# Page numbers for the cache reads held in SBUF, read from there by the sync engine

## The chip, the cores and the metric

The kernel runs on one core of a Trainium2 chip. The metric is the time of the whole program on the device, in microseconds, as the median of several runs. The engines are named as in the profile: PE (matrix products; PEld its weight loads), DVE (vector), ACT (scalar), POOL (general purpose) and SP (sync, which here does nothing but wait and issue DMAs; its rows carry the name SPq). Sixteen DMA engines move the data.

## The reference, cut to what matters

A two-layer decoder trunk works on 256 prompt tokens and 8 sample tokens with the same weights. In each layer a normalised input is projected by one wide matrix; one branch is a state space scan, the other latent attention; their gated sum goes through `w_out`, and a retrieval of single-neuron experts (PEER) follows. What matters here is the attention of the samples, each of which reads 2048 past positions out of a paged cache:

```python
past_lat = cache_latent[l][page_table].reshape(bs, past_len, KV_LORA)
past_kr = cache_krope[l][page_table].reshape(bs, past_len, QK_ROPE)
...
s = (jnp.einsum('bqhr,btr->bhqt', ql, kv) + jnp.einsum('bqhd,btd->bhqt', qp, kr)).astype(jnp.float32) * ATTN_SCALE
p = jax.nn.softmax(jnp.where(mask, s, -jnp.inf), axis=-1).astype(kv.dtype)
return jnp.einsum('bhqt,btr->bqhr', p, kv)
```

`page_table` has 8 rows (samples) of 16 page numbers, int32, in HBM. It is the same for both layers.

## The kernel before

A first block loads the constants, the inputs and a norm row, and all engines meet at a barrier. Then a loop over the two layers runs, each layer one block in which the five engines go through programs written out by hand and meet only by semaphores. So on each engine the order of the code is the order of execution.

**The sync engine's program of a layer.** It issues the loads of all weights into `wring`, a ring of two blocks: `load_block` waits on `blocks_begun`, which PE raises with the first product of each block, since the block before it is then no longer read. `block_of(w_in, GATE_B, k)` loads the last four of the input projection's 1 MB blocks; between them stand the first cache reads. The past of a sample is read in two halves, so there are `HALVES` = 16 of them, of `HALF_PAGES` = 8 pages each. A page is one DMA of 128 rows of 2176 bytes (272 KB) into `held`, a part of `arena` with three slots (`HELD` = 3); half i goes into slot i % 3. Before its eight DMAs `half_numbers(i)` reads the half's eight page numbers into registers of the sync engine, and for i from 3 on the engine then waits until PE has done the values of half i - 3, which frees the slot:

```python
for i in range(HELD, HALVES):
    if i in SSM_LOADS:
        block_of(w_ssm, 0, SSM_LOADS[i])
    numbers = half_numbers(i)
    sp.wait_ge(sem("aux_full"), marks["values", i - HELD])
    half_pages(i, numbers)
```

Half 0 begins after the wait on `el_used` (with the gate blocks), half 1 follows, and half 2 begins after the wait on `ring_free`, when the arena's last user before attention is done. The registers are loaded from HBM: the compiled program has, for each half, a load of the table's address (shown as `in_page_table_ptr`), a register addition where the half isn't the first, and one load of the eight numbers (`in_page_table`). These are the rows of L2027; the page DMAs are L2034, the weight blocks L2003.

**PE in the same stretch.** It does the gate products (L485 from `ht_tok,wring`), some turns and products, and then for each half `half_scores(i)` (L861 and L865, after the half's pages have landed), pieces of prompt attention and of the SSM projection (L485 from `arena,wring`), and `half_values(i)` (L886). Then come the attention's output products, `w_out`, and PEER, whose rows POOL gathers by indirect DMA (L2154) in a stretch of some 690 us per layer. POOL also moves the samples' SSM states in and out (L2126, L2132) while PE does the gate products.

Of the kernel before, what the change touches and what calls it, by code (L numbers as in the profile page):

```python
# [11 lines left out]
I32 = mybir.dt.int32  # L12
U32 = mybir.dt.uint32

D_MODEL, SEQ, DEPTH, SAMPLES = 1024, 256, 2, 8
# [5 lines left out]
PAGES = PAST // PAGE  # L21
# [26 lines left out]
HALF_PAGES = PAGES // 2  # L48
# [232 lines left out]
def build(nc, layers, a, out):  # L281

    (o_yp, o_ys, o_latp, o_krp, o_ssmp, o_convp, o_lats, o_krs, o_ssms, o_convs) = out
    a = dict(a, next_norm=a["norms"][1:DEPTH + 1, :])
    with ExitStack() as ctx:
        def sb(name, cols, dt=F32):
            return ctx.enter_context(nc.sbuf_tensor(name, [P, cols], dt))
# [3 lines left out]
        def sem(name):  # L291
            if name not in sems:
                sems[name] = ctx.enter_context(nc.semaphore(name))
            return sems[name]
# [48 lines left out]
        ysm = sb("ysm", DC * SAMPLES)  # L343
        att = sb("att", 96)
        layer_off = sb("layer_off", 2)
        arena = sb("arena", max(A1 + 2048, A3))
        ps = ctx.enter_context(nc.psum_tensor("ps", [P, 8, 512], F32))

# [99 lines left out]
        with nc.Block() as block:  # L448
            @block.sync
            def _(sp):  # L450
                sp.dma_start(consts[:, :], a["consts"]).then_inc(sem("first_loads"), 16)
                sp.dma_start(x[:, 0:2, :], a["x_prompt"].rearrange("o (t p) d -> p (o t) d", p=P)).then_inc(sem("first_loads"), 16)

                sp.dma_start(nrow[:, :], a["norms"][0, :].partition_broadcast(P)).then_inc(sem("first_loads"), 16)
                sp.wait_ge(sem("x_zeroed"), 1)
                sp.dma_start(x[0:SAMPLES, 2, :], a["x_sample"].rearrange("b o d -> (b o) d")).then_inc(sem("first_loads"), 16)
                sp.wait_ge(sem("first_loads"), 16 * 4)

            @block.vector
            def _(dve):  # L460
                dve.memset(x[:, 2, :], 0.0).then_inc(sem("x_zeroed"), 1)
                dve.memset(fwd[:, :], 0.0)
                dve.memset(layer_off[:, :], 0.0).then_inc(sem("off_zeroed"), 1)
# [3 lines left out]
        with nc.Fori(0, layers) as layer:  # L467
            with nc.Block() as block:
# [1525 lines left out]
                def _(sp):  # L1994
# [28 lines left out]

                    def half_numbers(i):

                        s = i // 2
                        return nc.values_load_multi_w_load_instructions(  # L2027
                            a["page_table"][s:s + 1, (i % 2) * HALF_PAGES:(i % 2 + 1) * HALF_PAGES], engines=(mybir.EngineType.SP,),
                            min_val=0, max_val=a["pages"].shape[1] - 1, skip_runtime_bounds_check_because="page numbers lie in the pool")[1]

                    def half_pages(i, numbers, some=range(HALF_PAGES)):
# [25 lines left out]
                    block_of(w_in, GATE_B, 1)  # L2057
                    sp.wait_ge(sem("el_used"), 1)
                    numbers = half_numbers(0)
                    half_pages(0, numbers, range(0, 2))  # L2060
                    half_pages(0, numbers, range(2, 4))
                    block_of(w_in, GATE_B, 2)
                    half_pages(0, numbers, range(4, 6))
                    block_of(w_in, GATE_B, 3)
                    half_pages(0, numbers, range(6, 8))
                    half_pages(1, half_numbers(1))
                    block_of(w_ssm, 0, 0)
                    sp.wait_ge(sem("ring_free"), 1)
                    half_pages(2, half_numbers(2))
# [4 lines that stand above are left out]
# [176 lines left out]
```

## Time and profile before

| | |
|---|---|
| median of 3 runs | 2316.95 us (2314.4 to 2320.23) |
| the profiled execution's own time | 2312.3 us, of which the span of the profile is 2310.8 us |
| PE busy | 1953.5 us, 85% of the span |
| DVE busy | 1516.2 us, 66% |
| DMA | 744.48 MB, mean 322 GB/s |
| page reads | 256 DMAs of 272 KB, 128 per layer |

The profile is of one execution, 4.65 us shorter than the median. Layer 0 lies at about 10 to 1160 us of the span and layer 1 at 1160 to 2300 us; the gate products with the first page reads at 186 to 222 us and 1330 to 1366 us, and the sixteen halves at 261 to 392 us and 1404 to 1534 us.

### The profile page before, as it was taken

The numbers are of one execution on the slowest core, as the hardware profiler recorded it, in microseconds if no ns is written. First come the engines' busy times: TensorE is split into PE (matmuls) and PEld (weight loads), VectorE is DVE, ScalarE is ACT, GpSimd is POOL, SyncE is SP. The second block draws the span as 40 slices with busy tenths as digits, with TensorE's granted clock in tenths as the row PEclk, the third lists the DMA queues.
The fourth block names the chain that finished last, engine by engine and source line by source line (L and its number), as shares of the span: only waits on it lengthen the run. The fifth ranks groups of instructions, "written<-read, shape, count | busy, mean of one in ns | idle before, by whom it ended". The sixth has DMA issues, their size and how long they took to land. (4 is left out here: it accounts for less than half of the span.)

```text
span 2310.8 us, 26923 instructions
## 1 busy us (share of the span) xinstructions
PE 1953.5 (85%) x9174; PEld 1124.3 (49%) x9174; DVE 1516.2 (66%) x3832; ACT 458.5 (20%) x1378; POOL 643.0 (28%) x594
## 2 busy tenths in 40 slices
PE   7999888999898777777699998899988987787775
PEld 5887656744344322222278876566544442222221
DVE  3555434677787888788545544337678778888874
ACT  2244210122112111111022532101121121111111
POOL 0000000134444344445200000002344443544451
PEclk9999899999999999999999999999999999999998
DMA  5447489499999999999654466875999998999995
GB/s 187 149 133 260 137 289 323 146 398 417 421 421 420 419 368 422 421 421 411 291 183 136 146 223 206 275 272 207 398 416 421 421 421 370 419 421 421 421 414 240
DMA packets 188196, 744.48 MB, mean 322 GB/s; under 512 B 16338, under 2 KB 76170, under 8 KB 117376
## 3 DMA queue, kind: packets, MB, share of 16 engines
q0 software_dynamic: 83296, 582.18, 61.5%
q1 hardware_dynamic: 104752, 160.47, 20.7%
q8 instruction: 74, 1.21, 0.2%
q14 instruction: 74, 0.61, 0.1%
HBM read 731.33 MB, written 11.46 MB: 321 GB/s over the span
## 5 line engine op out<-in xcount | busy, mean ns | idle before, releaser
L1067 PE MATMUL ps<-arena 128*128 128x512 f32 (+1 forms) x2112 | 1013.8, 613 | 238.7 <-DVE arena L1645 232.9
L2154 POOL DMA_INDIRECT arena<-in_peer_uv,arena x528 | 607.9, 1151 | 864.7 <-PE ps L1067 704.3
L1636 DVE CUSTOM_DVE_ANT_0 arena<-arena,h 128x1024 f32<-128x1024 f32 x512 | 627.5, 1226 | 236.2 <-DMA arena<-in_peer_uv,arena 228.9
L1067 PEld LDWEIGHTS ps<-arena 128*128 128x128 f32 (+1 forms) x2112 | 366.4, 188 | 849.0 <-DVE arena L1645 529.2
L485 PE MATMUL ps<-ht_tok,wring 128*128 128x264 f32 (+2 forms) x1728 | 380.8, 377 | 8.8 <-DMA wring<-in_w_in 5.4
L485 PEld LDWEIGHTS ps<-ht_tok,wring 128*128 128x128 f32 x1728 | 312.3, 190 | 75.2 <-issue 18.2
L1950 ACT ACTIVATE arena<-arena 128x1 f32<-128x1 f32 x528 | 105.8, 203 | 1031.3 <-DVE arena L1636 1030.5
L1645 DVE TENSOR_SCALAR arena<-consts,arena 128x128 f32<-128x128 f32 (+1 forms) x528 | 181.6, 344 | 20.6 <-ACT arena L1950 20.6
L2135 POOL DMA_DIRECT2D nrow<-in_norm_ffn x2 | 1.1, 533 | 334.2 <-PE ps L824 334.2
L485 PE MATMUL ps<-arena,wring 128*128 128x264 f32 (+2 forms) x512 | 91.8, 336 | 0.8 <-DVE arena L1420 0.8
L485 PEld LDWEIGHTS ps<-arena,wring 128*128 128x128 f32 x512 | 77.0, 191 | 10.3 <-DVE arena L1420 1.3
L494 PE MATMUL ps<-consts,h 128*128 128x128 f32 (+2 forms) x174 | 36.2, 315 | 31.4 <-DVE h L1165 27.8
L485 PE MATMUL ps<-wring,ht_tok 128*128 128x272 f32 (+5 forms) x288 | 59.4, 365 | 0.0
L485 PE MATMUL ps<-arena,gate 128*128 128x256 f32 x256 | 57.2, 382 | 2.2 <-DVE gate L1427 2.2
L886 PE MATMUL ps<-arena 128*32 128x256 f32 x512 | 36.0, 401 | 21.0 <-DVEq L1445 21.0
L485 PEld LDWEIGHTS ps<-arena,gate 128*128 128x128 f32 x256 | 48.1, 191 | 9.5 <-DVE gate L1427 2.6
L1292 DVE SCALAR_TENSOR_TENSOR h<-h,exs,arena 128x1024 f32<-128x1024 f32 x16 | 20.6, 1285 | 49.0 <-ACT arena L1825 49.0
L494 PEld LDWEIGHTS ps<-consts,h 128*128 128x128 f32 (+2 forms) x174 | 26.4, 173 | 48.8 <-DVE h L1165 29.4
L2126 POOL DMA_DIRECT2D out<-h x16 | 8.5, 534 | 148.9 <-DVE h L1292 148.9
L485 PEld LDWEIGHTS ps<-wring,ht_tok 128*128 128x128 f32 (+1 forms) x288 | 42.2, 161 | 15.6 <-issue 2.6
L861 PE MATMUL ps<-arena 128*32 128x256 f32 x512 | 37.1, 411 | 11.5 <-DVEq L1370 6.0
L1950 ACT ACT_TABLE_LOAD x36 | 46.2, 1283 | 0.6
(319 smaller groups left out, 1744.7 us busy)
## 6 DMA issues: line engine op xcount, KB each, us to landing
arena<-in_pages SPq DMA_DIRECT2D x256, 272.0 KB, 4.0
wring<-in_w_in SPq DMA_DIRECT2D x38, 1024.0 KB, 5.9
wring<-in_peer_wq SPq DMA_DIRECT2D x18, 1024.0 KB, 9.5
arena<-in_peer_uv,arena POOLq DMA_INDIRECT x528, 12.5
h<-in_state_ssm POOLq DMA_DIRECT2D x16, 512.0 KB, 5.1
out<-h POOLq DMA_DIRECT2D x16, 512.0 KB, 5.0
wring<-in_w_ssm_proj SPq DMA_DIRECT2D x8, 1024.0 KB, 8.2
arena<-in_w_out SPq DMA_DIRECT2D x8, 1024.0 KB, 14.9
```

Source lines behind the costliest of these rows:

```text
L485: last = pe.matmul(dst, w(c), rhs(c), start=start and c == 0, stop=stop and c == chunks - 1)
L494: return pe.transpose(dst, src, ident[0:rows, 0:rows])
L861: pe.matmul(ps[32 * g:32 * g + 32, b, 0:256], qs[:, s, c, :], held[:, slot, 2 * g:2 * g + 2, c * P:(c + 1) * P], start=c == 0, stop=False, ...
L886: last = pe.matmul(ps[32 * g:32 * g + 32, b, 0:KV_LORA], pts[:, i % 2, j, g, :], held[:, slot, 2 * g + j, 2 * P + ROPE:KV_ROW], start=j == ...
L1067: last = pe.matmul(ps[0:outs, SUM_BANK[t] + half, :], diag[:, n % DIAGS, 0:outs], ring[:, HOME[n % RING], D_MODEL + half * 512:D_MODEL + ( ...
L1292: dve.scalar_tensor_tensor(out=new, in0=new, scalar=exs[:, SAMPLES + s:SAMPLES + s + 1], in1=stx[:, s % 2, :, :], op0=ALU.mult, op1=ALU.ad ...
L1636: dve.tensor_tensor_reduce(ring[:, HOME[k], 0:D_MODEL], ring[:, HOME[k], 0:D_MODEL], tokens, 1.0, 0.0, ALU.mult, ALU.add, dots[:, column(n ...
L1645: dve.tensor_scalar(diag[:, n % DIAGS, 0:outs], table[:, 0:outs], gel[:, column(n)], wexp[:, column(n)], ALU.mult, ALU.mult).then_inc(sem( ...
L1950: act.activation(gel[:, at:at + 1], dots[:, at:at + 1], ACT.Gelu).then_inc(sem("gelu_ready"), 1)
L2126: pool.dma_start(h1[b], places[b % PLACES]).then_inc(sem(f"state_store{b % PLACES}"), 16)
L2135: pool.dma_start(nrow[:, :], of_layer("norm_ffn", layer).partition_broadcast(P)).then_inc(sem("ffn_row_load"), 16)
L2154: pool.indirect_dma_start(ring[:, HOME[k], :], None, table, bass.IndirectOffsetOnAxis(ap=idx[:, TOPK * u + j:TOPK * u + j + 1], axis=0)).t ...
```

## The change

The kernel gets an SBUF tensor `numbers` of 128 int32 per partition, of which partition 0 is used. The first block loads the whole page table (128 numbers, 512 bytes) into it by one more DMA, ahead of the samples' input, and waits for it with the other first loads. `half_numbers(i)` reads its eight numbers from SBUF.

```diff
+        numbers_held = sb("numbers", SAMPLES * PAGES, I32)
         arena = sb("arena", max(A1 + 2048, A3))
...
                 sp.dma_start(nrow[:, :], a["norms"][0, :].partition_broadcast(P)).then_inc(sem("first_loads"), 16)
+                sp.dma_start(numbers_held[0:1, :], a["page_table"].rearrange("(o s) k -> o (s k)", o=1)).then_inc(sem("first_loads"), 16)
                 sp.wait_ge(sem("x_zeroed"), 1)
                 sp.dma_start(x[0:SAMPLES, 2, :], a["x_sample"].rearrange("b o d -> (b o) d")).then_inc(sem("first_loads"), 16)
-                sp.wait_ge(sem("first_loads"), 16 * 4)
+                sp.wait_ge(sem("first_loads"), 16 * 5)
...
                     def half_numbers(i):
 
-                        s = i // 2
                         return nc.values_load_multi_w_load_instructions(
-                            a["page_table"][s:s + 1, (i % 2) * HALF_PAGES:(i % 2 + 1) * HALF_PAGES], engines=(mybir.EngineType.SP,),
+                            numbers_held[0:1, i * HALF_PAGES:(i + 1) * HALF_PAGES], engines=(mybir.EngineType.SP,),
```

What the sync engine's program holds in the first block, before (`ISA` in such listings is a short register instruction, `DMA` the issue of a transfer):

```order
L451 DMA consts<-in_consts 128x1428
L452 DMA x<-in_x_prompt 128x2x1024
L454 DMA nrow<-in_norms 128x1024
L456 DMA x<-in_x_sample 8x1024 [waits x_zeroed]
L448 UNCONDITIONAL_BRANCH [waits first_loads]
```

and with the change:

```order
L452 DMA consts<-in_consts 128x1428
L453 DMA x<-in_x_prompt 128x2x1024
L455 DMA nrow<-in_norms 128x1024
L456 DMA numbers<-in_page_table 1x128
L458 DMA x<-in_x_sample 8x1024 [waits x_zeroed]
L449 UNCONDITIONAL_BRANCH [waits first_loads]
```

One DMA issue stands ahead of the samples' input. The other place is the step from one half to the next on the sync engine, here from the last page of half 2 to the first of half 3, before:

```order
L2034 DMA arena<-in_pages 128x544
L2027 TENSOR_LOAD in_page_table_ptr
L2027 REGISTER_ALU
L2027 TENSOR_LOAD in_page_table
L2034 ISA [waits aux_full]
```

and with the change:

```order
L2035 DMA arena<-in_pages 128x544
L2028 TENSOR_LOAD numbers
L2035 ISA [waits aux_full]
```

Two loads and an addition have become one load, in each of 32 such steps. On the other engines nothing has moved.

## Rows read from the trace of the kernel before

**Rows 1.** The page: DMA share in tenths, 40 slices of the span

```profile
DMA  5447489499999999999654466875999998999995
```

**Rows 2.** PE's waits for transfers (us, times, longest): 186:222, 1330:1366, 185:410, 1404:1534

```profile
PE ps L485 <- DMA wring<-in_w_in: 3.1, 1, 3.1
...
PE ps L485 <- DMA wring<-in_w_in: 2.1, 1, 2.1
...
PE ps L861 <- DMA arena<-in_pages: 4.2, 3, 1.7
...
PE ps L861 <- DMA arena<-in_pages: 1.2, 2, 0.9
```

**Rows 3.** The sync engine's waits, whole span

```profile
SPq L2034 <- PE ps L886: 0.5, 1, 0.5
```

**Rows 4.** L2027, whole span: duration ns min/median/max, first and last start

```profile
L2027 SPq TENSOR_LOAD <-in_page_table_ptr x32: 832/2522/4115, 190.0 to 1512.6; - x32
L2027 SPq TENSOR_LOAD <-in_page_table x32: 887/899/2475, 192.6 to 1514.5; - x32
L2027 SPq ALU_OP  x30: 37/38/58, 212.9 to 1514.5; - x30
```

**Rows 5.** L2027 in 189:194, 215:264, 264:272 and 280:287

```profile
L2027 SPq TENSOR_LOAD <-in_page_table_ptr x1: 2591/2591/2591, 190.0 to 190.0; - x1
...
L2027 SPq TENSOR_LOAD <-in_page_table_ptr x1: 837/837/837, 258.0 to 258.0; - x1
...
L2027 SPq TENSOR_LOAD <-in_page_table_ptr x1: 2652/2652/2652, 264.5 to 264.5; - x1
L2027 SPq TENSOR_LOAD <-in_page_table x1: 893/893/893, 267.3 to 267.3; - x1
...
L2027 SPq TENSOR_LOAD <-in_page_table_ptr x1: 3933/3933/3933, 281.8 to 281.8; - x1
```

**Rows 6.** Sync engine's timeline: half 3 alone; halves 2 to 4; half 3's landing

```profile
268.40 4.67 SPq L2034 DMA_DIRECT2D arena<-in_pages  x8
...
260.20 20.96 SPq L2034 DMA_DIRECT2D arena<-in_pages  x24
...
DMA to landing us min/median/max: 2.7/3.9/5.0
```

**Rows 7.** DMA in stretches: us, busy of five engines, PEclk, DMA share, GB/s

```profile
193.00:195.00 2.00, 2.00 (x10) 1.72 (x10) 0.71 (x1) 1.18 (x5) 0.00 (x0) 1.00 0.44 114
201.00:206.00 5.00, 2.78 (x13) 2.05 (x11) 3.65 (x3) 1.56 (x6) 1.06 (x2) 1.00 1.05 361
...
276.00:278.00 2.00, 2.00 (x60) 1.48 (x52) 0.82 (x2) 0.00 (x0) 0.00 (x0) 1.00 0.36 100
...
2.00:8.00 6.00, 0.00 (x0) 0.00 (x0) 0.47 (x3) 0.00 (x0) 0.00 (x0) 1.00 1.01 366
```

**Rows 8.** Sync engine's timeline, 185:330, at the gate blocks

```profile
188.59 0.54 SPq L2003 DMA_DIRECT2D wring<-in_w_in  x1
193.80 2.04 SPq L2034 DMA_DIRECT2D arena<-in_pages  x4
196.50 0.56 SPq L2003 DMA_DIRECT2D wring<-in_w_in  x1
```

**Rows 9.** PE's timeline: start, us, what, [idle before, ended by]; both layers

```profile
280.95 1.05 PE L861 MATMUL ps<-arena 128*32 128x256 f32 x16
...
305.14 1.07 PE L861 MATMUL ps<-arena 128*32 128x256 f32 x16 [1.73 <-DMA arena<-in_pages]
...
383.39 1.07 PE L861 MATMUL ps<-arena 128*32 128x256 f32 x16 [1.70 <-DMA arena<-in_pages]
...
391.48 0.39 PE L911 MATMUL ps<-arena,latt 128*8 128x64 f32 x4
...
1525.36 1.07 PE L861 MATMUL ps<-arena 128*32 128x256 f32 x16 [0.29 <-DMA arena<-in_pages]
...
1533.44 0.39 PE L911 MATMUL ps<-arena,latt 128*8 128x64 f32 x4
```

## The prediction

> **What bounds the kernel now.** I read the page first. The DMA share is 9 in the long gather stretches of PEER and in the attention slices of both layers [rows 1]. The change touches nothing in PEER, so the question is what the sync engine's page reads cost PE. The list of waits, cut to the stages, answers it: PE waits for pages 4.2 us in layer 0 (three times, 1.7 at most, at halves 6, 8 and 15; the first of these is in [rows 9]) and 1.2 us in layer 1, and once per layer for a gate block of `w_in`, 3.1 and 2.1 us, at the place where page reads stand between the weight loads [rows 2]. Together that is 5.4 + 5.2 = 10.6 us. This is the most that page reads can give back, 0.46% of the time.
>
> Why do pages come late? The sync engine's own waits show it: for a slot to be freed it waited once in the whole run, 0.5 us [rows 3]. In all other steps the slot had been free, and the engine itself came late. Its timeline says with what: eight page issues take 4.67 us, but three halves take 20.96 us from first issue to last, so two steps of (20.96 - 3 x 4.6) / 2, about 3.6 us, lie between them [rows 6]. They are the register loads: a median of 2.52 us for the address, 0.04 for the addition and 0.90 for the numbers, with gaps 3.6 [rows 4].
>
> Is a wait of PE passed on to the end? Half 15 began after a wait of 1.70 us in layer 0 and of 0.29 us in layer 1, and from there to L911 behind the last half it took 8.09 us (391.48 - 383.39) and 8.08 us (1533.44 - 1525.36) [rows 9]. So nothing behind the wait had used it. After attention everything hangs on PE's products until the first expert numbers, and the gathers follow from them. I pass it on one to one.
>
> **The change part by part.**
>
> *The load's new length.* It is not in this trace; bounds come from the loads that are. The address load took 0.84 us after the engine's long wait for `ring_free`, 2.65 us right behind eight page issues, and 3.93 us behind a 1 MB weight block; the numbers load that followed the second of these, from the same memory under the same traffic, took 0.89 us [rows 5]. So it isn't the reading that is long but being the first read behind DMA issues: about 1.7 us of it looks like a wait until those issues have got through. The new load is now the first read. Lower bound 0 (an SBUF read might cost next to nothing and wait for nothing), upper bound 4.1 us, the longest address load [rows 4]. I take 2.5 us behind pages, the address load's median, because it takes that load's place, and 0.84 after idleness. Then a step saves the second load, the addition and their gaps, 1.0 us of 3.6; with a load of 0.84 it would save 2.8.
>
> The Trainium skill's page "DMA: Bandwidth & Descriptors", section "Latency and other measured facts", gives HBM access 0.2 us on average and 2 us at high load, and a floor of some 600 ns for such a register load. By it the first load would be long because HBM is busy, and one from SBUF would be back in 0.6 us, saving 3.0 us a step; the sum below would stay, and the last two rivals would lose most of their chance. The trace disagrees as to the cause: the second load reads HBM just as busy and takes 0.89 [rows 5].
>
> *What an earlier issue gains in attention.* The DMA engines set a floor. Half 3 was issued from 268.40 on; its last page landed 5.0 us after an issue near 272.7, so at about 277.7, while half 4's first issue was at about 276.9 (one period of 8.5 later). Between them the engines idled: in 276 to 278 us their share was 0.36, so 1.3 us of idleness in a period of 8.5, [rows 6, 7]. With the idleness gone a half needs 7.2 us. A 1 MB weight block at 361 GB/s [rows 7] adds 2.9 us, and three of them stand among halves 3 to 15. PE, without its waits, goes from half 3 to half 15 in 383.39 - 280.95 - 4.2 = 98.2 us [rows 2, 9]. The engines' floor for the same twelve steps is 12 x 7.2 + 3 x 2.9 = 95.1 us, and half 3 already lies there 3.2 us ahead of PE (280.95 - 277.7). So the floor is below PE's need by 6 us at the end; the tightest places are halves 6 and 8, behind weight blocks. Half 6 could have landed at 277.7 + 3 x 7.2 + 2.9 = 302.2 and is wanted at 305.14 - 1.73 = 303.4 [rows 9]: 1.2 us are left. The lead must also be made: one microsecond saved per step gives 3 to 4 by half 6, where 1.7 is wanted, and more than 10 by half 15, where 4.2 is; some is lost in waiting for slots at halves 3 and 4. So I expect nearly all of the page waits to go: 5.0 of 5.4 us. What is late next in those places is DVE's part between the products, which stands in the trace anyway and moves along with PE.
>
> *The gate blocks.* The block issued at 196.50 is the one PE waits for 3.1 us. Its issue hangs on PE's own start of a block, and I leave it there; what can change is how much is queued ahead of it. Four pages are issued ahead of it from 193.80 on, after the loads that begin at 190.0 [rows 5, 8]. In 193 to 195 us the DMA share is 0.44, so 1.1 us of engine time is lost there, and until the block has landed the engines are full (1.05 in 201 to 206) [rows 7]. Pages issued 1.0 us earlier fill this hole and let the block land that much earlier; more than 1.1 us can't be won, as the previous block's transfer lies before it, unless the full stretch shortens by other means. Bounds: 0 and 3.1 us in layer 0, 0 and 2.1 in layer 1. I take 1.15 each, 2.3 us.
>
> *The added DMA.* One more issue, about 0.5 us, stands ahead of the samples' input. In 2 to 8 us the engines are full with the constants and the prompt (1.01) [rows 7], and the input's 32 KB comes behind them in any case, so the cover is 5 us deep; 512 bytes more are nothing. 0 us, and 0.5 if the cover were gone. The new tensor moves the arena by 512 bytes per partition, 0.
>
> **Sum:** 5.0 + 2.3 - 0 = 7.3 us. The profiled execution's own time of 2312.3 us becomes 2305.0. The median of the runs shown is 4.65 us above it, and I give the time on that scale: 2316.95 - 7.3 = 2309.7 us, 0.31% less.
>
> **The rivals.**
>
> 1. *The gate waits go as a whole.* Then 5.4 + 5.2 = 10.6 us, 2306.4. For it: the load may be back 1.7 us sooner than I take. Against it: only 1.1 us of idle engine time lies there [rows 7]. Chance 0.13.
> 2. *The DMA floor catches the gain.* Pages issued sooner only queue longer; one or two waits behind weight blocks stay, and POOL's state transfers take the hole ahead of the gate block. For it: 6 us of slack in 98, about 1 at halves 6 and 8. Then 3 to 5 us, 2312 to 2314. Chance 0.22.
> 3. *The change doesn't shorten the step.* If the new load returns only when the pages have passed, at the moment the numbers load returns now, nothing is won: 2317. For it: the first load's length follows what was issued ahead of it; against it: in each case shown the numbers load takes its own 0.9 on top. Chance 0.08.
> 4. *Slower: the load from SBUF takes longer than the whole step does now*, because it competes with page writes into the same memory. It decides from 3.6 us on. Every period is already the sync engine's, so 4.1 us, the upper bound, costs 0.5 x 12 steps x 2 layers = 12 us: 2329. For it only that the reading side isn't in the trace; against it the 0.84 and 0.89 us of plain reads. Chance 0.07.
>
> **How the numbers follow.** My forecast has 0.50, with 5.5 to 9 us. From no change this kernel can be told by about 0.3%, 7 us. Rival 1 and somewhat over half of the forecast's chance lie beyond: faster 0.45. The rest of the forecast with rivals 2 and 3 is the same: 0.48. Rival 4 is slower: 0.07. The range leaves out rival 4 and most of rival 3: from rival 1 less 1 us, 2305.5, to 2316.0. The forecast's own is 2307.5 to 2312.
>
> **What would show it.** In the profile after: one register load per half, about 2.5 us behind pages and 0.8 at half 2; the step between halves about 2.6 instead of 3.6 us. SP waits for slots (L2035 for PE) not once but in many halves, several us in all. PE's waits for pages under 0.5 us, for the gate block about 2 and 1 us. The first barrier at the same time. The DMA share between halves up from 0.36. I am wrong if the load is over 3.6 us, if waits for pages stay at halves 6 and 8, or if the time falls by less than the waits do, so that something behind attention had the slack.

## The result, and the profile after

| | before | after |
|---|---|---|
| median of four runs | 2316.01 us (2314.4 to 2320.23) | 2297.77 us (2289.79 to 2302.48) |
| ratio | | 0.9905, 95% interval 0.9884 to 0.9925 |
| profiled execution, span | 2310.8 us | 2288.3 us |
| mean granted clock of that execution | 0.980 | 0.985 |

The kernel became faster by 18 us; forecast were 7.3. The profiled execution is the fastest of the four and 8 us below their median, so its 22.5 us of difference in span are more than the change typically gives.

The register loads come first. The groups of L2028, whole span, with duration in ns as min/median/max; they answer to [rows 4]:

```profile
L2028 SPq TENSOR_LOAD <-numbers x32: 521/526/735, 189.2 to 1486.0; - x32
```

One load of 0.53 us stands where there were 2.52 + 0.04 + 0.90 and their gaps. From the end of half 0's last page issue to the start of half 1's first, both layers show 0.78 us. Even right behind page issues the load is short. The longest, 0.735 us, is the very first.

What the sync engine and PE wait for (us in total, times, longest), the first two over the whole span, the last two in 186:222 and 1320:1366:

```profile
SPq L2035 <- PE ps L888: 65.5, 24, 5.3
...
SPq L449 <- DMA x<-in_x_sample: 6.3, 1, 6.3
...
PE ps L487 <- DMA wring<-in_w_in: 1.0, 1, 1.0
...
PE ps L487 <- DMA wring<-in_w_in: 0.7, 1, 0.7
```

The sync engine waited for a slot once and 0.5 us before [rows 3]; now it waits 24 times and 65.5 us: it runs ahead of PE. PE has no wait for pages left in either layer, where it had 4.2 and 1.2 us, and its gate-block waits fell from 3.1 and 2.1 us [rows 2] to 1.0 and 0.7. The 10.6 us of waits for transfers in these places are now 1.7. The first barrier's wait is no longer than before (6.3 us against 6.5).

At the gate blocks, the sync engine's timeline (start, us), and then DMA in stretches (us, busy of five engines, PEclk, DMA share, GB/s):

```profile
187.80 0.54 SPq L2005 DMA_DIRECT2D wring<-in_w_in  x1
190.20 2.04 SPq L2035 DMA_DIRECT2D arena<-in_pages  x4
195.70 0.56 SPq L2005 DMA_DIRECT2D wring<-in_w_in  x1
```

```profile
193.00:195.00 2.00, 2.00 (x11) 1.71 (x10) 1.41 (x2) 0.38 (x2) 0.00 (x0) 1.00 1.05 390
...
2.00:8.00 6.00, 0.00 (x0) 0.00 (x0) 0.48 (x3) 0.00 (x0) 0.00 (x0) 1.00 0.99 367
```

The four pages begin 3.6 us earlier than in [rows 8] (the whole program is 0.8 us ahead here), and the hole of share 0.44 [rows 7] is filled: 1.05. The block that PE waits for is issued 0.8 us earlier, as PE itself is, and comes sooner: from its issue to PE's first product with it 10.4 us passed before (196.50 to 206.88) and 8.3 after (195.70 to 204.01).

These waits are 8.9 us. The other part of the difference has its own sign in the trace. PE between gates and attention, before and then after (start, us, what, [idle before, ended by]):

```profile
231.03 5.45 PE L494 MATMUL ps<-consts,arena 128*128 128x128 f32 x24 [1.87 <-DVEq L1326]
236.41 7.31 PE L485 MATMUL ps<-cqt,arena 128*128 128x264 f32 x24
```

```profile
228.16 4.25 PE L496 MATMUL ps<-consts,arena 128*128 128x128 f32 x24 [1.87 <-DVEq L1328]
232.34 5.61 PE L487 MATMUL ps<-cqt,arena 128*128 128x264 f32 x24
```

The same products take 2.9 us less, with no transfer near. The row of a stretch of before says why: the granted clock was 0.50, the lower of its two levels, 1.2 instead of 2.4 GHz, with PE busy throughout:

```profile
233.10:239.90 6.80, 6.80 (x21) 4.64 (x22) 2.62 (x7) 3.82 (x7) 0.00 (x0) 0.50 0.00 0
```

So two things changed: waits for transfers, and time at the lower clock. The experiments ask whether the second belongs to the change, and through what.

### The profile page after: what moved, and what is told of

The parts are those of the page before. It is cut to its first block and busy times, and to the rows that moved or that the text cites. A ratio compares the mean times of both kernels' runs of the same rounds, so it can differ in the third digit from the quotient of the medians.

```text
span 2288.3 us, 26862 instructions
## 1 busy us (share of the span) xinstructions
PE 1941.2 (85%) x9174; PEld 1117.7 (49%) x9174; DVE 1516.4 (66%) x3832; ACT 458.8 (20%) x1378; POOL 648.7 (28%) x594
## 5 line engine op out<-in xcount | busy, mean ns | idle before, releaser
L888 PE MATMUL ps<-arena 128*32 128x256 f32 x512 | 35.8, 399 | 21.0 <-DVEq L1447 21.0
L487 PEld LDWEIGHTS ps<-wring,ht_tok 128*128 128x128 f32 (+1 forms) x288 | 41.2, 158 | 15.3 <-issue 2.6
L1945 ACT ACT_TABLE_LOAD x34 | 43.6, 1283 | 0.8
```

The source lines that it names most:

```text
L487: last = pe.matmul(dst, w(c), rhs(c), start=start and c == 0, stop=stop and c == chunks - 1)
L888: last = pe.matmul(ps[32 * g:32 * g + 32, b, 0:KV_LORA], pts[:, i % 2, j, g, :], held[:, slot, 2 * g + j, 2 * P + ROPE:KV_ROW], start=j == ...
L1945: act.activation(w, w, ACT.Exp, accum_out=wsum[:, u % 2:u % 2 + 1]).then_inc(sem("experts_exp"), 1)
```

## The experiments

All ratios are against the kernel before on the same chip. "Gate wait" is PE's wait for a gate block in layer 0 and 1, "page wait" its waits for pages, from the profiled execution; the clock is the median over the runs of that kernel. The kernel before ran in six sessions, with a median clock of 0.975 in four of them, 0.976 beside gate_order_hbm and 0.974 beside the last pair, and with median times of 2317.23 to 2321.89 us.

| run | ratio, 95% | median us | gate waits | page waits | clock |
|---|---|---|---|---|---|
| after_again | 0.9931 (0.9914 to 0.9947) | 2299.38 | 1.0, 1.3 | 0 | 0.979 |
| after_third | 0.9918 (0.9900 to 0.9935) | 2299.16 | 0.7, 0.8 | 0 | 0.981 |
| gates_only | 0.9975 (0.9962 to 0.9989) | 2311.58 | 0.6, 0.6 | 1.7, 3.6 | 0.978 |
| attention_only | 0.9957 (0.9939 to 0.9975) | 2307.36 | 2.9, 2.5 | 0 | 0.979 |
| step_kept_long | 0.9944 (0.9926 to 0.9962) | 2303.43 | 0.9, 2.0 | 0 | 0.979 |
| step_longer | 0.9988 (0.9974 to 1.0002) | 2318.30 | 3.3, 3.8 | 0.4, 1.0 | 0.975 |
| loaded_only | 0.9996 (0.9984 to 1.0008) | 2318.31 | 3.9, 3.1 | 1.6, 2.2 | 0.975 |
| pages_after_gates | 0.9904 (0.9885 to 0.9922) | 2300.01 | 0.7, 0.2 | 0 | 0.980 |
| pages_after_gates_again | 0.9916 (0.9898 to 0.9934) | 2297.64 | 0.5, 0.7 | 0 | 0.981 |
| gate_order_hbm | 0.9981 (0.9965 to 0.9997) | 2313.72 | 0.6, 0.4 | 0.8, 0.9 | 0.976 |
| before_filled | 1.0031 (1.0017 to 1.0044) | 2324.57 | 0.2, 0 | 0, 0.3 | 0.974 |
| after_filled | 1.0034 (1.0021 to 1.0047) | 2327.45 | 0 | 0 | 0.974 |
| early_steps_long | 0.9927 (0.9902 to 0.9952) | 2300.04 | 0.8, 1.0 | 0 | 0.980 |
| late_steps_long | 0.9913 (0.9886 to 0.9940) | 2297.32 | 0.7, 0.8 | 0 | 0.982 |
| early_from_hbm | 0.9936 (0.9915 to 0.9957) | 2307.60 | 0.3, 0.2 | 1.2, 0.3 | 0.976 |
| late_from_hbm | 0.9904 (0.9880 to 0.9929) | 2297.84 | 0.8, 1.3 | 0 | 0.982 |

**The changed kernel again, and its two parts.** The edit of the parts, in which the other halves read HBM as before (`i < 2` for gates_only, `i >= 2` for attention_only):

```diff
+                        s = i // 2
+                        held_row = numbers_held[0:1, i * HALF_PAGES:(i + 1) * HALF_PAGES]
+                        table_row = a["page_table"][s:s + 1, (i % 2) * HALF_PAGES:(i % 2 + 1) * HALF_PAGES]
...
-                            numbers_held[0:1, i * HALF_PAGES:(i + 1) * HALF_PAGES], engines=(mybir.EngineType.SP,),
+                            held_row if i < 2 else table_row, engines=(mybir.EngineType.SP,),
```

after_again:

> The changed kernel once more. In its profile 8.9 us less of waits for transfers are seen and about 24 us less of time at the half clock, which would be worth up to 12 us. Theory 1 (the shorter step keeps PE supplied, and the fuller PE is granted the full clock in stretches where it was halved before): 0.992 of before again, 2297 us, and a second profile again without the half-clock stretch that before has at 233 us and 1376 us, just behind the gate blocks. Theory 2 (the clock differed by chance between two profiles): 0.996, some 2307 us, and the half-clock stretches come and go.

gates_only:

> Only halves 0 and 1, which stand among the gate blocks, read their numbers from SBUF; halves 2 to 15 read HBM as before. Theory 1: the waits for the gate block fall from 3.1 and 2.1 us to about 1.0 and 0.7, and the half-clock stretch of 6.8 us behind them goes in both layers (3.4 us each of PE time at most, 2.9 as the two profiles show); page waits stay at about 5: 3.5 + 5.8 = 9.3 us less, 0.996, 2307 us. Theory 2: only 3.5 us, 0.9985.

attention_only:

> Only halves 2 to 15 read SBUF; halves 0 and 1 read HBM as before. Theory 1: page waits go (5.4 us), the gate waits of 3.1 and 2.1 us and the half clock behind them stay: 0.9977, 2310.5 us. Theory 2: the same 5.4 us. A third theory, that the page-number reads from HBM cost something beyond the sync engine's lateness, would give more than 8 us here.

Against the 2318.26 us of before in that session the whole change gave 0.69%, 16.0 us; the gate part 0.25%, 5.8 us; the attention part 0.43%, 10.0 us. The parts add up. The attention part is more than the waits in its place: 5.4 us of page waits gave 10.0 (interval 5.8 to 14.1). At the gates 4.0 of 5.2 us of waits went and 5.8 us of time (interval 2.6 to 8.8), so there the time alone doesn't show that more than the waits was gained. More than 8 us in attention is also what the third theory asked for, that a read of HBM costs beyond its length; the next runs decide on it.

**Is it the length of the step?** step_kept_long reads from SBUF too, but in seven loads instead of one, which brings the step to about 2.5 us; step_longer takes longer loads still, 3.7 us; loaded_only keeps the new tensor and its DMA and reads HBM throughout (`held_row if False else table_row`).

```diff
+                        out = []
+                        for first, count in ((0, 1), (1, 1), (2, 1), (3, 1), (4, 1), (5, 1), (6, 2)):
+                            at = i * HALF_PAGES + first
+                            out += list(nc.values_load_multi_w_load_instructions(
+                                numbers_held[0:1, at:at + count], engines=(mybir.EngineType.SP,),
...
```

and for step_longer, where `read(first, count)` loads `count` numbers from SBUF:

```diff
...
+                        if i == 2:
+                            return read(0, 2) + read(2, 2) + read(4, 2) + read(6, 2)
+                        return [read(k, 2)[0] for k in range(6)] + read(6, 2)
```

step_kept_long:

> The numbers come from SBUF, but each half reads them by seven loads (six of one number, one of two) in place of one, at 0.53 us each, so that the step stays at about 3.7 us as before, with no read of HBM. Theory 1 (the length of the step is all): the time of before, 2313 to 2317 us, with page waits of about 5 us and gate waits of 2 to 3 us per layer. Theory 3 (it is the read of HBM behind DMA issues, not its length): the time of the changed kernel, 2298 us.

step_longer:

> As step_kept_long, where single numbers took only 0.27 us each, so that its step was 2.2 us and not 3.7. Here each of seven loads reads two numbers (0.46 us each), which makes the step some 3.4 us, with no read of HBM; half 2 reads with four loads. Theory 1 (the length of the step is all): close to before, 0.998, 2313 us, with page waits of 3 to 5 us. Theory 3 (the read of HBM costs beyond its length): 0.993 to 0.995 as the changed kernel and step_kept_long.

loaded_only:

> The table is loaded into SBUF with the first loads and the tensor has its place, but all halves read their numbers from HBM as before. Theory 1: no difference from before, within 0.15%, the same waits. A fourth theory, that the shifted place of the arena or the first loads carry part of the gain: 3 us or more less.

Their loads in the trace, of step_kept_long, step_longer and loaded_only:

```profile
L2031 SPq TENSOR_LOAD <-numbers x224: 261/269/477, 188.9 to 1498.4; - x112
```

```profile
L2028 SPq TENSOR_LOAD <-numbers x218: 462/467/685, 189.5 to 1517.0; - x109
```

```profile
L2031 SPq TENSOR_LOAD <-in_page_table_ptr x32: 844/2546/4284, 190.0 to 1523.9; - x32
L2031 SPq TENSOR_LOAD <-in_page_table x32: 897/908/1882, 192.6 to 1526.0; - x32
```

With a step of 3.7 us and no read of HBM at all, step_longer is within 0.3% of before (0.9988), with gate waits and a clock like before's; its page waits were 1.4 us where 3 to 5 were expected. loaded_only is before (0.9996): tensor, DMA and the moved arena cost and bring nothing. step_kept_long was meant to keep the step of before and did not, because a load of one number takes 0.27 us; with its 2.5 us it gives 0.9944, most of the gain. So the time follows the step's length, and the memory read matters only through it: the third theory falls.

One more profiled execution of the kernel before shows how its executions differ:

> The kernel before, one more profile. The profiled execution of before took 2312.3 us where its runs have a median of 2316 to 2318, so it may show less of the waits than is usual. If the unexplained rest of the gain (16 to 18 us by the medians, 8.9 us by the waits of the two profiles) lies in the waits, this profile shows 10 to 15 us of PE's waits for transfers instead of 10.6; if it lies in the clock, the waits are again near 10.6 and the time at the half clock is longer than in profiles of the changed kernel.

Its 2312.81 us went with gate waits of 3.1 and 3.2 us, page waits of 2.7 and 1.3 us and a mean clock of 0.979. These waits are 10.3 us together, and loaded_only's, with before's reads, 10.8; so the 10.6 us of the first profile are usual, and the gain of 16 to 18 us is not explained by waits that it happened to miss.

**The gate waits by order alone.** In the changed kernel (pages_after_gates) and in the kernel before with its HBM reads (gate_order_hbm), all four gate blocks, and the first SSM block, are issued ahead of the pages of halves 0 and 1:

```diff
-                    block_of(w_in, GATE_B, 0)
-                    block_of(w_in, GATE_B, 1)
+                    for k in range(4):
+                        block_of(w_in, GATE_B, k)
                     sp.wait_ge(sem("el_used"), 1)
-                    numbers = half_numbers(0)
...
+                    half_pages(0, half_numbers(0))
+                    half_pages(1, half_numbers(1))
```

pages_after_gates:

> The changed kernel with one more step: all four last gate blocks and the first SSM block are issued first, and the pages of halves 0 and 1 only then, in the stretch from about 215 to 260 us where the engines have little to do. Theory 1: the waits for the gate block, about 1 us per layer, go as well, and with them what half clock may follow; 0.992 to 0.990 of before, some 2 us under the changed kernel. Against it: the pages of half 1 are done some 15 us later, which still is 10 us ahead of their use. If the gate wait is due to POOL's state transfers, it stays.

then its repetition, on one chip with the changed kernel (after_third):

> The changed kernel again, beside the next one: 0.992, 2299 us, clock 0.980.

> The changed kernel with the pages of halves 0 and 1 behind the gate blocks, again, to be compared with the changed kernel on the same chip. It saves 1 to 2 us of gate waits: 0.991, 1 to 3 us under the changed kernel; if its first ratio of 0.990 was chance, the same as the changed kernel.

gate_order_hbm:

> The kernel before, all page numbers read from HBM as there, and the step between halves left at 3.6 us; only the order at the gates changes: the four gate blocks and the first block of the SSM projection are issued ahead of the pages of halves 0 and 1. So the gate waits (3.1 and 2.1 us in the trace of before) should go to about 1 us each with no register read shortened. Theory 1 (every late transfer costs its wait in PE, and about as much again in time at the half clock): the run with halves 0 and 1 alone read from SBUF gave 0.9975; this one takes the same waits away, so 0.997 to 0.9985, clock 0.977 to 0.978, if halves 0 to 2 still land in time. Rival 6 (the part beyond the waits comes from the register reads themselves, or from the engine's idle time being spent in a semaphore wait instead of in a read of HBM): the gate waits go, but only 2 to 4 us of time with them and the clock stays at 0.975, ratio 0.9985 to 0.9995. Rival 7 (pages of halves 0 and 1 come too late behind the blocks): waits for pages grow by what the gate waits lose, and the time is within 0.1% of before.

On the changed kernel the new order is no faster that can be told: 2297.64 against 2299.16 us on one chip, with intervals that overlap. On the kernel before it gives 4.4 us (0.7 to 8.1) with every HBM read left, a little less than the gate part of the change (5.8, interval 2.6 to 8.8). The ratio lies where theory 1 had it (0.997 to 0.9985), but the clock did not rise to 0.977 as it said: it was 0.976 in both kernels, which is rival 6's forecast. Rival 6's 0.9985 to 0.9995 lies inside the interval too, so it isn't ruled out, and how much of the gate part is clock stays open.

**Is PE's idleness what lowers the clock?** Unused products (128x512) are put into PE's program where it used to wait, in both kernels:

```diff
+                    def fillers(b, count):
+
+                        for _ in range(count):
+                            pe.matmul(ps[:, b, :], ident, consts[:, 0:512], start=True, stop=True)
...
+                        if m == 20:
+                            fillers(b, 4)
...
+                        fillers(b, {6: 2, 8: 1, 9: 1}.get(i, 0))
```

before_filled:

> The kernel before, where PE does products whose result is not used at the places where it would mostly wait: 128x512 products of the constants into the bank that the next product overwrites, four ahead of the third pair of gate blocks and two, one and one ahead of the scores of halves 6, 8 and 9, in each layer; 8 x 0.61 us = 4.9 us of products per layer, against some 5.3 us of waits for transfers per layer. Nothing else changes. Theory 5 (the second half of the gain is the clock, which PE's idleness brings down): granted clock up from 0.975 to 0.978 or more by the median of the runs, and the time 3 to 7 us under before, though PE does more. Rival: the clock doesn't follow PE's idleness (or follows the transfers instead): clock 0.975, time 0 to 4 us over before.

after_filled:

> The changed kernel with the same unused products, as a control: here there is hardly a wait to fill, so nearly all of 9.8 us is added: 2299 + 8 = 2307 us, 0.996 of before. By theory 5 the clock stays at about 0.979 or rises by 0.001; if the products themselves lift the clock it rises as much as in the other run.

The waits for transfers in these places were gone in both (0.5 and 0 us in all), and both ran at 0.974 with 0.31 and 0.34% more time than before. The changed kernel lost 28 us (2327.45 - 2299.16). Its trace shows that the products were longer than planned. The two ahead of half 6 and the one ahead of half 8:

```profile
303.45 1.98 PE L521 MATMUL ps<-consts 128*128 128x512 f32 x4
...
322.28 1.12 PE L521 MATMUL ps<-consts 128*128 128x512 f32 x2
```

Each product is two records, and about 1 us of PE instead of 0.61: from the start of each group to PE's next product the sixteen take 14.9 us in all, where 9.8 were planned. The rest of the 28 us goes largely with the clock. The profiled execution had 123 us at half clock, after_third's 94; at the 0.36 to 0.41 us per microsecond found below, these 29 us cost 10 to 12 (an estimate). So the simple form of the theory, that PE's idle time lowers the clock and that more products would hold it up, fell: with the waits filled there was more time at half clock, not less.

**Where in attention the clock falls.** Thirteen profiles without added products can be compared stage by stage. From the first scores of half 0 to the last values of half 15 PE's stage takes, by the trace:

| attention stage | stages | us | of it at half clock | page and SSM waits |
|---|---|---|---|---|
| steps long up to half 6 (before, before_look, loaded_only, step_longer, gates_only, gate_order_hbm) | 12 | 129.2 to 133.5, mean 131.5 | 6.2 to 20.4 | 0.8 to 4.2, mean 1.9 |
| steps of 0.8 us (2.5 in step_kept_long) (after, after_again, after_third, both pages_after_gates, step_kept_long) | 12 | 125.7 to 126.0 | 6.5 to 7.1 | 0 |
| attention_only | 2 | 126.0 and 128.4 | 7.1 and 12.8 | 0 |

Long steps cost 5.6 us per layer, of which only 1.9 are waits. Most of the rest is time at the lower clock, and it has a fixed place. (A stage of the changed kernel has 3.3 to 3.6 us of it at its start and 3.4 us about 75 us on; the question is what the late stages have besides.) PE of step_longer (3.7 us steps) at half 6, and the same place in the changed kernel:

```profile
305.38 1.07 PE L863 MATMUL ps<-arena 128*32 128x256 f32 x16 [0.43 <-DMA arena<-in_pages]
306.27 0.63 PE L867 MATMUL ps<-arena 128*32 128x64 f32 x32
309.00 1.09 PE L496 MATMUL ps<-consts,arena 128*128 128x128 f32 x8 [2.10 <-DVE arena L1405]
309.93 3.17 PE L802 MATMUL ps<-latt,arena 128*128 128x256 f32 x8
```

```profile
297.52 1.05 PE L863 MATMUL ps<-arena 128*32 128x256 f32 x16
298.39 0.63 PE L867 MATMUL ps<-arena 128*32 128x64 f32 x32
301.12 1.09 PE L496 MATMUL ps<-consts,arena 128*128 128x128 f32 x8 [2.10 <-DVE arena L1405]
302.05 1.89 PE L802 MATMUL ps<-latt,arena 128*128 128x256 f32 x8
```

Both wait 2.10 us for DVE. Only the first waited 0.43 us for pages, for the product that begins 3.6 us earlier, and there the eight products behind it take 3.17 instead of 1.89 us. The two stretches, the same distance from the first scores, PEclk being the third number from the end:

```profile
310.40:313.80 3.40, 3.40 (x9) 2.30 (x8) 0.58 (x1) 0.00 (x0) 0.00 (x0) 0.50 1.00 341
```

```profile
302.90:306.30 3.40, 2.73 (x19) 1.61 (x21) 1.09 (x4) 0.00 (x0) 0.00 (x0) 1.00 1.04 383
```

A half-clock stretch begins 44 to 50 us behind the first scores in 11 of the 12 stages of the first line and in one (attention_only, layer 1) of the 14 others. Four kernels tested whether the wait for half 6 brings it. Two use step_longer's reads, two the HBM reads, each in halves 2 to 6 or in halves 7 to 15 alone; all other halves have the one short read. The edit of early_from_hbm, beside gates_only's line:

```diff
-                            held_row if i < 2 else table_row, engines=(mybir.EngineType.SP,),
+                            table_row if 2 <= i <= 6 else held_row, engines=(mybir.EngineType.SP,),
```

early_steps_long:

> The changed kernel, with the step before halves 2 to 6 of each layer lengthened to about 3.7 us by seven reads from SBUF; all other steps short (one read). Theory 8: in attention a short wait of PE for half 6, 3 us ahead of its fixed wait of 2.10 us for DVE, is what lets the granted clock fall there, some 47 us behind the first scores (11 of 12 profiled attention stages with late pages show this stretch, 1 of 14 with early ones). Then here a wait of 0.4 to 1.2 us at half 6 in both layers, a stretch at the half clock 44 to 50 us behind the first scores, no stretch about 100 us behind them, and an attention stage of 127.5 to 129 us where the changed kernel has 126; time 3 to 6 us above the changed kernel, ratio 0.993 to 0.995. Rival 8 (the clock falls by chance, or by the whole stage's pace, not behind this wait): the stage is 126 us plus the wait alone, no stretch there, ratio 0.9915 to 0.993. Rival 9 (five long steps are not enough to make half 6 late): stage 126, no wait, ratio as the changed kernel's.

late_steps_long:

> The same the other way round: halves 0 to 6 with one read and a short step, halves 7 to 15 of each layer with the step of about 3.7 us. Theory 8: half 6 is early, so no stretch at the half clock 44 to 50 us behind the first scores; the lead of the first halves also carries most of the later ones, so waits of 0 to 1.5 us at halves 12 to 15, attention stage 126 to 127.5 us, ratio 0.9915 to 0.9935, within 3 us of the changed kernel. Rival 8 (the stage's pace, that is the number of long steps, sets the half clock): nine long steps cost more than the other kernel's five, stage 128 to 130 us, ratio 0.994 to 0.997.

early_from_hbm:

> The changed kernel with the numbers of halves 2 to 6 of each layer read from HBM as before (the load behind a weight block was 4 us there), all others from SBUF. Now half 6 should be late as in the kernel before: a wait of 0.4 to 1.7 us for its pages. Theory 8 (this one wait, 3 us ahead of a fixed wait of 2.10 us, brings the clock down): a half-clock stretch 44 to 50 us behind the first scores in both layers, attention stage 128 to 130 us, ratio 0.993 to 0.9955. Rival 8 (the pace of the whole stage brings it): stage 126 us plus the wait (126.5 to 127.5), no stretch there, ratio 0.991 to 0.993.

late_from_hbm:

> The other way round: numbers of halves 7 to 15 from HBM, 0 to 6 from SBUF. Theory 8: half 6 is early, no stretch 44 to 50 us behind the first scores; waits of 0 to 1 us at half 12 or 15 at most, attention stage 126 to 127 us, ratio 0.990 to 0.993. Rival 8: stage 128 to 130 us with a half-clock stretch 98 to 103 us behind the first scores, ratio 0.9935 to 0.996.

In the first pair no wait for pages is listed (rival 9): stages of 126.1 and 126.2, 125.9 and 125.8 us, no extra stretch. In early_steps_long half 6 was only just late: its scores begin 42.4 and 42.5 us behind the first scores, 42.2 to 42.3 in the changed kernel. In early_from_hbm half 6 was late. PE's waits of early_from_hbm in the attention stages of layers 0 and 1, then these stages and the stretch behind half 6:

```profile
PE ps L863 <- DMA arena<-in_pages: 1.2, 2, 0.9
...
PE ps L863 <- DMA arena<-in_pages: 0.3, 1, 0.3
```

```profile
259.90:392.60 132.70, 116.41 (x1366) 81.06 (x1366) 47.02 (x121) 18.99 (x73) 0.42 (x1) 0.92 0.87 294
1406.80:1536.40 129.60, 113.89 (x1366) 79.84 (x1366) 46.94 (x121) 19.00 (x73) 0.45 (x1) 0.95 0.90 301
308.00:311.40 3.40, 3.40 (x13) 2.86 (x11) 1.38 (x2) 0.00 (x0) 0.00 (x0) 0.51 1.03 368
```

and late_from_hbm, with HBM reads in nine of sixteen steps:

```profile
259.60:385.50 125.90, 110.03 (x1366) 76.55 (x1366) 46.74 (x121) 19.00 (x73) 0.45 (x1) 0.97 0.90 303
1395.80:1521.70 125.90, 110.06 (x1363) 76.86 (x1364) 46.61 (x120) 19.01 (x73) 0.26 (x1) 0.97 0.91 305
```

Waits of 1.2 and 0.3 us went with stages that are 6.7 and 3.6 us longer than 125.9. The number of products is the same (1366), and PE was busy 6.4 and 3.8 us longer with them, because the clock was at half 48 and 99 us behind the first scores, in both layers, though the steps behind half 6 were short. late_from_hbm has none of it: nine HBM reads per layer cost nothing. On the same chip the two medians are 9.8 us apart (2307.60 and 2297.84). The intervals of their two ratios just overlap, but four of the first kernel's five times (2307.32 to 2312.35) lie above all four of the second (2296.24 to 2301.70), and the fifth, 2300.59, above three of them. Rival 8 falls: not the stage's pace but lateness at half 6. Theory 8 holds in its direction; layer 0's stage is longer than the 128 to 130 us that it gave.

A listed wait is not the whole lateness. In layer 1 of early_from_hbm the scores of half 6 begin 43.1 us behind the first scores, 0.9 us later than in the changed kernel, where 0.3 us is listed: some 0.2 us beyond each wait, and half 5 was a little late too.

Over all 34 stages, the extra stretch followed in 12 of the 13 in which PE waited for half 6, and in 2 of the 21 in which it didn't. Layer 0 of the profiled execution before waited 1.73 us there [rows 9] without the stretch (gates_only's layer 0 waited 1.72 with it), and layer 1 of before and of attention_only had the stretch without the wait. The three exceptions have something in common. A half-clock stretch lies across the first scores in every stage; in these three it begins 7.5 to 7.7 us ahead of them, as in one more stage (layer 1 of loaded_only, 7.8, which waited and had the extra stretch). In the other 30 it begins 6.3 to 7.2 us ahead, and there wait and extra stretch go together without exception: 11 with both, 19 with neither. So it seems to matter also when the clock's changes fall relative to PE's program. This was seen in the traces afterwards and not tested.

## Why the prediction was wrong

**The step that failed** is in the first part: "I pass it on one to one", and with it "10.6 us. This is the most that page reads can give back". The argument behind it ([rows 9]: 8.09 and 8.08 us from half 15 to L911) looked only for slack that would swallow a wait. It could not show that a wait costs more than its length, and in the profiled execution the stretch behind half 6 was missing in layer 0. The sum had no term for the clock. In 14 stages (the 12 with long steps and early_from_hbm's two) the mean is 131.4 us, 5.5 above the changed kernel's 125.9: 1.8 us of waits, and 8.5 us more at the lower clock (15.3 against 6.8). Over the single stages the rest beyond the waits is 0.41 us per extra microsecond at half clock (a fit through zero, worked out from the 14 and attention_only's second), so 3.5 us. A second fit, over all 34 stages, that also counts what each wait costs beyond its listed length gives 0.3 us for each wait and 0.36 for the clock, so 3.1 us. Either way the waits are the smaller part. The Trainium skill, page "TensorE: Matmul & The Clock Gate", section "HAM oscillation — how this bites in real kernels", counts the penalty of such time as half of it. The 0.36 to 0.41 found here are somewhat less. The same section of the Trainium skill attributes the falls of the clock in a thin kernel to its waits for DMA, of about 3 to 5 us each. The runs agree that late transfers bring falls, but here listed waits of 0.3 to 1.7 us, followed by the fixed one of 2.1, were enough. The further thought that more work for PE would keep the clock up is not borne out by the filled kernels.

**The gate blocks** were the other term set too low: 2.3 us forecast, 2.1 + 1.4 = 3.5 us of waits gone in the profiled execution and 5.8 us of time (2.6 to 8.8) in gates_only. The bound of 1.1 us of idle engine time that was held against rival 1 was too tight: the pages began 2.8 us earlier relative to PE, and the block's way from issue to use shortened by 2.1 us. Here too there is a clock part, as the rows of 231 to 244 us show: where a half-clock stretch begins 27 to 31 us ahead of the first scores, the way to them from PE's last product of L564 (L566 after), which lies behind the gate waits, is 42.0 to 43.6 us instead of 39.2, so 2.8 to 4.4 us longer. But that stretch stands in layer 0 in four of the five profiles with gate waits of 2.9 us and more (not in before_look) and in seven of the twelve with short ones that have no added products; in layer 1 it is in all five and in six of the twelve. So its tie to the gate wait is a tendency, and no run tests it.

**The load's length.** Taken were 2.5 us behind pages; it is 0.53, and the step 0.8 instead of 2.6 us. The reason given, that the first read waits for the DMA issues ahead of it on its engine, fails for a read of SBUF: this load stands in the same place and doesn't wait. The long times go with the address load from HBM (0.83 to 4.28 us), and what it waits for stays open, since the second HBM load takes 0.90 in the median. The sentence of the Trainium skill that was set beside it ("DMA: Bandwidth & Descriptors", "Latency and other measured facts", some 600 ns) was the better estimate. The trace has 0.53. In attention this error cost the forecast nothing, and that is luck of a kind: a step of 2.5 us is enough to empty the waits, as step_kept_long shows, so the forecast's 2.6 and the real 0.8 do the same.

**Page waits**: 5.0 of 5.4 us forecast to go, 5.4 gone; the tightest places were named, halves 6 and 8, and the argument from the DMA floor held: halves landed in time everywhere. **Slots**: the sync engine waits in 24 of the 26 halves that need one, as foreseen. **The added DMA**: nothing, shown by loaded_only and by the first barrier's 6.3 us. **The rivals**: 2 and 3 (the floor, no shortening) and 4 (slower) did not occur; rival 1 came nearest but counted waits alone. The range's lower end, rival 1 less 1 us, rested on the same "at most", and the measured 2297.77 us lies below it. The range given for the forecast alone, 2307.5 to 2312, is half a microsecond wider at each end than its 5.5 to 9 us; nothing hung on that.

**What stays open.** Why PE's lateness at half 6 often lets the clock fall later in the stage too; why three stages of 34 go against it, for which the position of the clock's changes is only a guess; and the falls between the gates and attention. The filled kernels had 118 and 123 us at half clock without waits for pages and gate blocks, against 95 in before and 94 in after_third, and one of their four stages (layer 0 of before_filled) had the extra stretch with no half late; theory 8 by itself does not explain that. From the stages, attention accounts for about 11 us of the change's 16 to 18 and the gates for the rest.

## What to carry to other kernels

When a short wait is to be removed, look beyond its length: compare how long the same number of products takes behind it, and read the granted clock of that stretch, in several executions. The sum of waits is then not the most that can be gained; here a listed wait of 0.3 us at one place (0.9 us by the starts of the products) went with 3.6 us of time. A sync engine that never waits for a slot is itself the pace of the stage, and each register load between its DMAs counts; once it has a lead, even slow loads are free (late_from_hbm). So look for the first place where the lead runs out, here half 6 behind a weight block: steps ahead of it cost time only when they make that place late (early_from_hbm did, early_steps_long hardly). And when products are put in as a test, read from the trace how long they took.

## What the runs showed of the hardware

A register load from SBUF took 0.27 us for one number, 0.47 us for two and 0.53 us for eight, also right behind DMA issues of the same engine. From HBM eight numbers took 0.90 us (median; 2.48 at most), and the load of the address ahead of them 0.83 to 4.28 us (median 2.5). The granted clock fell for stretches of 3.4 us and more with PE busy in all of the stretch (3.40 of 3.40 us at 0.50), behind a wait of 0.43 us followed by one of 2.10 us, and held behind the 2.10 us alone; and added products that took 15 us of PE cost 28 us, with the clock at 0.974 instead of 0.981. A 128x512 product of float32 constants stood in the trace as two records of 0.59 us and took PE about 1 us.
